# One compressed-attention step a head, staging in the middle of a head, and a scan whose K updates run on VectorE

## The chip, the cores and the metric

The kernel runs on one NeuronCore of a Trainium2 chip. The metric is the device time of one execution in microseconds (us). TensorE (PE) multiplies, VectorE (DVE) and ScalarE (ACT) work elementwise on SBUF and PSUM, GpSimd (POOL) elementwise on SBUF, and SyncE (SP) issues the loads. The engines run their own instruction streams and meet only through semaphores.

## The reference

Two transformer-like blocks run one after the other on a sequence of 512 tokens with 1024 features, all in float32. The first block has a gated feed-forward layer, then a mixed attention, then a second feed-forward layer and a gated embedding. Its attention is what the change touches first: eight "NSA" heads with three branches each (compressed, selected, window) and eight "forgetting" heads.

```python
# compressed branch: 31 blocks of 32 tokens, one key and value per block
s_c = jnp.einsum('bkgqd,bknd->bkgqn', qq, k_cmp) * scale
p_c = masked_softmax(s_c, m_c) * m_c
o_c = jnp.einsum('bkgqn,bknd->bkgqd', p_c.astype(v_cmp.dtype), v_cmp)
...
return gg[..., 0:1] * o_c + gg[..., 1:2] * o_s + gg[..., 2:3] * o_w
```

With 512 tokens there are eight blocks to select and all are taken, so that the selected and the window branch are both plain causal attention over their own keys.

The second block puts 16 meta tokens ahead (528 positions) and runs a gated linear recurrence over them, eight heads of 128:

```python
S_new = jnp.exp(G_last[:, :, 0, :])[..., None] * S + jnp.einsum('bhsd,bhsv->bhdv', k_dec, vb)
```

With decay f, keys are K = 1 - f and the output is a causal sum over earlier positions, each weighted by the product of the decays between them.

## The kernel before

**Layout.** Activations lie transposed, features on the 128 partitions and tokens in the free dimension. Each weight unit is split into two float32r parts: `whi`, made by ScalarE (`hi`, L731), and `wlo`, made by GpSimd in pieces of 128x512 (`lo`, L639). The order of every engine's stream is written out by hand; there is no planner.

**The attention loop** (one loop over `STEPS` in the stream of each engine) has a step for every head n, query block i of 128 queries, and branch b: 0 selected, 1 window, 2 compressed, `FOX` (3) forgetting. That is 8x4x4 = 128 steps. TensorE does in turn s the score of step s (L2093 to L2101), the transposes of the probabilities of step s-2 (L2114, L2117), and the product with the values of step s-4 (L2127, L2131). VectorE takes the row maximum of step s (L1401) and adds up the output of step s-5 into `otok` (L1426 to L1432; the reciprocals and the gates are L1417 and L1419). ScalarE does the exponential (L995) and copies the transposed probabilities to `probT` (L1017, L1019). Scores, transposes and outputs have three, three and two PSUM banks.

A compressed step has 32 keys: a mask product, two score products with `kch` of 32 columns, one transpose to 32 partitions and a product whose operands `probT` and `vcmp` have 32 partitions. A forgetting step has one more score product (L2099), whose operands `negsel` and `csplit` have 40 partitions; it puts the cumulated forget gates on the scores.

**Staging.** Queries and forgetting keys of head n+2 are split into two parts beside the last block of head n: `stage_q` and `stage_fox_q` on ScalarE (L887, L891), `stage_fox_k` (two copies, L1274) and `stage_fox_c` (L1278) on VectorE in one go, the rest on GpSimd (L669, L678).

**The scan** does the recurrence in levels. At level lv, blocks of 2^lv positions are joined in pairs: TensorE forms K transposed times Q for each head (L2248, from level 7 on L2251 and L2254), VectorE selects the part of that level into `Ad` with a predicated copy (L1609, at level -1 L1612), multiplies Q with decays (L1629), and halves the table of decays (L1635, `Tod` and `Tev` in turn); GpSimd multiplies K with decays (L720). The eight heads go as two groups of four. K itself is made by VectorE in one instruction (L1591). The 16 meta positions have small instructions of their own (L1604, L1641 to L1651). The results of levels 7 and 8 are copied by ScalarE (L1099).

Of the kernel before, what the change touches and what calls it, by code (L numbers as in the profile page):

```python
# [6 lines left out]
F32R = mybir.dt.float32r  # L7
# [6 lines left out]
P = 128  # L14
D = 1024
KD = D // P
S = 512
# [88 lines left out]
FOX = 3  # L106
STEPS = [(n, i, b) for n in range(NH) for i in range(TT) for b in (0, 1, 2, FOX)]
# [16 lines left out]
def slot(s):  # L124

    return s % 12
# [19 lines left out]
def level_updates():  # L146

    n, out = 1, {}
# [19 lines left out]
LEVEL_CP0 = sum(lv < 7 for lv, _, _ in LEVEL_SEQ)  # L168
# [6 lines left out]
def build(nc, a, out):  # L175
    ctx = ExitStack()
    with ctx:
# [76 lines left out]
        vcmp = at("vcmp", [32, NKV, HD], R2 + 42752)  # L254
# [10 lines left out]
        negsel = at("negsel", [FL0 + NH, 4, P], AR + U_VW * S * 4, F32R)  # L265
        csplit = at("csplit", [FL0 + NH, S], AR + U_VS * S * 4, F32R)
# [128 lines left out]
        nmax_done = sem("nmax_done")  # L395
        exp_done = sem("exp_done")
# [39 lines left out]
        lev_k = sem("lev_k")  # L436
        amx_mm = sem("amx_mm")
# [193 lines left out]
        def _(pool):  # L631
# [83 lines left out]
            for lv in range(LEVELS - 1):  # L715
                for g in range(2):

                    pool.wait_ge(lev_mm, 1 + max(i for i, (l, n, _) in enumerate(LEVEL_SEQ) if l == lv and n in range(HG * g, HG * (g + 1))))
                    k2, decay = k_update(lv, g)
                    nc.gpsimd.tensor_tensor(k2, k2, decay, ALU.mult).then_inc(lev_k, 1)  # L720
# [4 lines left out]
        def _(act):  # L725
# [220 lines left out]
            act.wait_ge(cmp_mm, 3)  # L946
            nc.scalar.activation(kcsq[:], ps[:, SMALL_BANK, HID0:HID0 + 64], ACT.Square).then_inc(cmp_sq, 1)
            nc.scalar.activation(vcmp[:], ps[0:32, SMALL_BANK, HID0 + 64:HID0 + 192].rearrange("p (g d) -> p g d", g=NKV), ACT.Copy).then_inc(cmp_sq, 1)
# [3 lines left out]
            act.wait_ge(cmp_mm, 4)  # L952
# [9 lines left out]
            nc.scalar.activation(kch[:, 0, :], kcmp[:], ACT.Copy).then_inc(k_hi, 1)  # L962
            nc.scalar.activation(warm[:, 0:1], epsc[:], ACT.Exp).then_inc(warmed, 1)
# [17 lines left out]
            SQ_HEADS = 4 * TT * (NH - 1)  # L981
            SQ0 = SQ_HEADS + LAG_O + 1
            LAST_AT = [SQ_HEADS + 4 * i + LAG_O + 5 - i // 2 for i in range(3)]

            def last_square(n):
                head_square(n, NH - 1, NH, SQ_HEADS + (n // 2 + 1) * 4)

            for s in range(NS + LAG_T):
                if s < NS:
                    n, i, b = STEPS[s]  # L990
                    w = 32 if b == 2 else (i + 1) * P
# [7 lines left out]
                    if i == TT - 1 and n + 2 < NH:  # L999
                        if b == 2:  # L1000
                            stage_q(n + 2)
                        if b == FOX:
                            stage_fox_q(n + 2)
# [1407 lines left out]
```

## Time and profile before

| | us |
|---|---|
| median of 3 runs | 2267.65 |
| lowest and highest | 2264.34, 2269.47 |
| the profiled execution | 2270.92 |
| its span | 2269.1 |

| engine | busy us | share of the span |
|---|---|---|
| PE | 2197.0 | 97% |
| POOL | 931.7 | 41% |
| DVE | 872.5 | 38% |
| ACT | 751.5 | 33% |

In order of time the attention loop lies from 563 to 749 us and the scan from 1687 to 1786 us. What lies around them is projections and feed-forward layers. A busy share says only how long instructions of an engine ran, and not whether they set the time; this is read in each stage from what the engine waited for. The starts of two neighbouring instructions of an engine, one taken from the other, give what the first costs in a full stream; the duration in a row also holds its latency, in which the next one already runs. The granted clock of TensorE is 1.00 at 2.4 GHz and 0.50 at 1.2 GHz.

### The profile page before, as it was taken

The page shows a single profiled execution, that of the slowest core. Times are in us where ns is not written, and L with a number is a line of the kernel's source. Part 1 is how long each engine was busy: PE and PEld are TensorE (multiplying, and loading weights), DVE is VectorE, ACT ScalarE, POOL GpSimd, SP SyncE. Part 2 cuts the span into 40 slices and gives each one's busy share as a digit, 9 for nine tenths or more (in the row PEclk, how much of TensorE's full clock was granted, in tenths as well). Part 3 has the DMA queues.
Part 4 walks back from the last instruction along what each step waited for, and adds up shares of the span by engine and source line. Part 5 has one row for each costly group of instructions (what it writes and reads, how often), then busy time and mean ns, then how long its engine had stood idle before and what let it go on. Part 6 is the DMA issues. An engine that isn't in the chain of part 4 may idle for free.

```text
span 2269.1 us, 32814 instructions
## 1 busy us (share of the span) xinstructions
PE 2197.0 (97%) x12844; PEld 1910.1 (84%) x12844; DVE 872.5 (38%) x1296; ACT 751.5 (33%) x1153; POOL 931.7 (41%) x707
## 2 busy tenths in 40 slices
PE   8999999999999999999999999999988899999998
PEld 6788888777888778887887999999988798989887
DVE  4222202676555432223016322232229554565402
ACT  4333222435666533334124432212210333333213
POOL 3444444435221344444444444444334324454442
PEclk9999999999999999999999999999999999999999
DMA  5323222522000222222322222222210012222321
GB/s 157 94 91 107 87 102 93 151 65 75 1 2 1 65 90 77 93 92 93 111 93 75 75 93 92 87 84 89 93 57 1 20 38 85 83 96 89 105 98 56
DMA packets 152174, 178.98 MB, mean 79 GB/s; under 512 B 6949, under 2 KB 142478, under 8 KB 152094
## 3 DMA queue, kind: packets, MB, share of 16 engines
q1 hardware_dynamic: 151931, 177.83, 24.1%
q8 instruction: 55, 0.90, 0.2%
q14 instruction: 25, 0.20, 0.0%
q10 hardware_dynamic: 163, 0.04, 0.0%
HBM read 175.76 MB, written 2.10 MB: 78 GB/s over the span
## 4 chain that ended last, share of the span: by engine, by line
PE 62%; issue 22%; POOL 11%; DVE 3%; DMA 1%; ACT 0%; SPq 0%; POOLq 0%; DVEq 0%; ACTq 0%
PE ps L1723 40%; POOL wlo L639 11%; PE ps L1863 11%; PE ps L2225 3%; PE ps L2248 2%; PE ps L2131 2%; PE ps L2101 2%; PE ps L2117 1%; PE ps L1975 1%; DVE tmp L1161 1%; DMA raw<-in_ffn_wu 1%; DVE Ad L1609 0%; PE ps L2127 0%; PE ps L2099 0%; PE ps L2182 0%
## 5 line engine op out<-in xcount | busy, mean ns | idle before, releaser
L639 POOL TENSOR_TENSOR wlo<-raw,whi 128x512 fp32r<-128x512 f32 x634 | 831.9, 1344 | 1123.7 <-ACT whi L731 1119.3
L1723 PE MATMUL ps<-xh,whi 128*128 128x512 f32 (+2 forms) x2432 | 703.0, 335 | 10.4 <-POOL wlo L639 8.8
L1723 PE MATMUL ps<-xh,wlo 128*128 128x512 f32 (+2 forms) x2432 | 700.6, 334 | 0.0
L1723 PE MATMUL ps<-xl,whi 128*128 128x512 f32 (+2 forms) x2432 | 697.6, 333 | 0.0
L731 ACT ACTIVATE whi<-raw 128x2048 fp32r<-128x2048 f32 (+1 forms) x158 | 301.1, 1906 | 772.7 <-PE ps L1723 466.8
L1723 PEld LDWEIGHTS ps<-xh,whi 128*128 128x128 f32 x2432 | 415.1, 189 | 62.8 <-POOL wlo L639 10.1
L1723 PEld LDWEIGHTS ps<-xh,wlo 128*128 128x128 f32 x2432 | 414.0, 189 | 46.9 <-issue 1.9
L1723 PEld LDWEIGHTS ps<-xl,whi 128*128 128x128 f32 x2432 | 413.9, 189 | 45.9
L1863 PE MATMUL ps<-act_h,whi 128*128 (+1 forms) x528 | 209.2, 396 | 0.0
L1863 PE MATMUL ps<-act_l,whi 128*128 (+1 forms) x528 | 208.9, 396 | 0.0
L1863 PE MATMUL ps<-act_h,wlo 128*128 (+1 forms) x528 | 208.2, 394 | 0.0
L1220 DVE SCALAR_TENSOR_TENSOR h<-ps,h 128x512 f32<-128x512 f32 x24 | 16.4, 685 | 307.8 <-PE ps L1863 307.3
L1863 PEld LDWEIGHTS ps<-act_l,whi 128*128 128x128 f32 x528 | 99.6, 189 | 23.3
L1863 PEld LDWEIGHTS ps<-act_h,wlo 128*128 128x128 f32 x528 | 99.6, 189 | 23.0
L1863 PEld LDWEIGHTS ps<-act_h,whi 128*128 128x128 f32 x528 | 99.6, 189 | 22.2
L777 ACT ACTIVATE act_h<-tmp 128x512 f32 (+1 forms) x66 | 41.8, 633 | 209.9 <-DVE tmp L1210 209.9
L1207 DVE TENSOR_TENSOR tmp<-ps,rbs 128x512 f32<-128x512 f32 x66 | 45.4, 688 | 148.6 <-PE ps L1723 148.6
L1401 DVE TENSOR_REDUCE stat<-ps 128x1 f32<-128x32 f32 (+4 forms) x128 | 53.0, 415 | 79.4 <-PE ps L2101 78.7
L1188 DVE TENSOR_TENSOR tmp<-ps,rbs 128x512 f32<-128x512 f32 x44 | 30.2, 691 | 135.6 <-PE ps L1723 135.2
L2248 PE MATMUL ps<-Q,K 128*128 128x128 f32 x512 | 65.8, 294 | 15.4 <-DVE Tod L1635 6.4
L995 ACT ACTIVATE prob<-ps,stat 128x32 f32<-128x32 f32 (+4 forms) x128 | 59.7, 466 | 61.8 <-DVE stat L1401 61.4
L2248 PEld LDWEIGHTS ps<-Q,K 128*128 128x128 f32 x512 | 64.2, 208 | 16.6 <-DVE Tod L1635 6.6
(312 smaller groups left out, 2556.0 us busy)
## 6 DMA issues: line engine op xcount, KB each, us to landing
raw<-in_w_in SPq DMA_DIRECT2D x47, 1024.0 KB, 5.1
raw<-in_ffn_wg SPq DMA_DIRECT2D x22, 1024.0 KB, 5.3
raw<-in_ffn_wu SPq DMA_DIRECT2D x22, 1024.0 KB, 5.3
raw<-in_ffn_wd SPq DMA_DIRECT2D x22, 1024.0 KB, 4.9
raw<-in_w_up SPq DMA_DIRECT2D x22, 1024.0 KB, 5.0
raw<-in_w_down SPq DMA_DIRECT2D x11, 1024.0 KB, 4.9
raw<-in_w_out SPq DMA_DIRECT2D x8, 1024.0 KB, 4.9
raw<-in_ple_w_gate SPq DMA_DIRECT2D x4, 1024.0 KB, 5.0
```

The source lines that it names most:

```text
L639: last = nc.gpsimd.tensor_tensor(wlo[:, slot, d], raw[:, slot, d], whi[:, slot, d].bitcast(F32), ALU.subtract)
L731: nc.scalar.activation(whi[:, slot, 0:n], raw[:, slot, 0:n], ACT.Copy).then_inc(hi_ready, 1)
L777: nc.scalar.activation(act_h[:, bass.ds(2 * i + j, 1), :], tmp[:, 2 + j:3 + j, 0:S], ACT.Copy).then_inc(acth_done, 1)
L995: nc.scalar.activation(prob[:, s % 3, 0:w], ps[:, s % 3, 0:w], ACT.Exp, bias=stat[:, 0, slot(s):slot(s) + 1], accum_out=stat[:, 1, slot(s) ...
L1207: nc.vector.tensor_tensor(tmp[:, 2 + j, 0:S], ps[:, 4 + 2 * j if conv else 2 + j, :], rbs[:, M:T], ALU.mult).then_inc(up_scaled, 1)
L1401: nc.vector.tensor_reduce(stat[:, 0, slot(s):slot(s) + 1], ps[:, s % 3, 0:w], AX_X, ALU.max, negate=True).then_inc(nmax_done, 1)
L1723: last = mm(ps[:, j * banks + b, 0:n], w[:, k, e * P:(e + 1) * P], x[:, k, c0:c0 + n], start=(k == 0 and q == 0), stop=(k == KD - 1 and q ...
L1863: last = mm(ps[:, n, :], w[:, e, n * P:(n + 1) * P], x[:, bass.ds(k + e, 1), :].rearrange("p a s -> p (a s)"), start=(start and e == 0 and ...
L2101: last = mm(out_, q_[:, e, i * P:(i + 1) * P], keys[x], start=False, stop=(x == 1), skip_group_check=True)
L2131: last = mm(o, probT[:, q % 3, k, :], vtok[:, k, v0:v0 + 2 * HD], start=(k == 0), stop=(k == i))
L2225: last = mm(ps[:, 3 * (u % 2) + g // 2, g % 2 * UC:(g % 2 + 1) * UC], x[:, k, c0:c0 + P], w[:, k, :], start=(k == 0 and q == 0), stop=(k = ...
L2248: last = mm(ps[:, bank, i * P:(i + 1) * P], K[:, n, xc(i)], Q[:, n, xc(i)], start=True, stop=True)
```

## The change

- The four compressed steps of a head become one, which goes first in the head (`PER_HEAD` is 13, so 104 steps). Its scores lie side by side in 128 columns (eight products of 32 columns and one mask product), VectorE takes four maxima at once, subtracts them from PSUM into `prob`, ScalarE takes one exponential in place, VectorE sums up in blocks, one transpose follows, and one product with `vcmp`, which now has 128 partitions and 256 columns with the values in four diagonal blocks and zeros elsewhere. It writes the compressed branch of all four query blocks to `otok` at once.
- `vcmp` is made by 16 small products in place of 4 in `compressed`, a clearing on VectorE that waits for `k_lo`, and four copies on ScalarE. `negsel` and `csplit` have 128 partitions in place of 40, those beyond filled with zeros.
- Head n+1 is staged inside head n: `stage_q` at step (1, 1), `stage_fox_q` at (2, 0), the two halves of `stage_fox_k` at (2, 1) and (2, FOX), `stage_fox_c` (for n+3) at (3, 0).
- In the scan K is made by ScalarE in two halves, the K updates are VectorE's, between the Q update and the table; TensorE no longer waits for the table; levels 5 and 6 are copied to `Ad` by ScalarE in blocks; GpSimd's next `lo` waits for the last scan product.

```diff
@@ attention, TensorE
-                    if b == 2:
-                        mm(out_, ident_b[:], cmpneg[:, i, :], start=True, stop=False, skip_group_check=True)
-                        keys = [kch[:, x, 32 * it:32 * it + 32] for x in range(2)]
+                    if b == CMP:
+                        mm(out_, ident_b[:], cmpneg[:].rearrange("p i k -> p (i k)"), start=True, stop=False, skip_group_check=True)
+                        for t in range(TT):
+                            for x in range(2):
+                                last = mm(out_[:, 32 * t:32 * t + 32], q_[:, e, t * P:(t + 1) * P], kch[:, x, 32 * it:32 * it + 32],
+                                          start=False, stop=(x == 1), skip_group_check=True)
...
-                    if b == 2:
-                        last = mm(o[:, 0:HD], probT[0:32, q % 3, 0, :], vcmp[:, n // 4, :], start=True, stop=True)
+                    if b == CMP:
+                        if n == 0:
+                            pe.wait_ge(vcmp_ready, TT)
+                        last = mm(ps[:, 6 + q % 2, 0:TT * HD], probT[:, q % 3, 0, :], vcmp[:, n // 4].rearrange("p i d -> p (i d)"),
+                                  start=True, stop=True)
@@ attention, VectorE
+                    if b == CMP:
+                        blocks = lambda x: x.rearrange("p (i k) -> p i k", i=TT)
+                        cmax = cstat[:, 0, TT * (n % 2):TT * (n % 2 + 1)]
+                        nc.vector.tensor_reduce(cmax, blocks(ps[:, s % 3, 0:P]), AX_X, ALU.max, negate=True).then_inc(cmax_done, 1)
+                        dve.wait_ge(cmax_done, n + 1)
...
+                        nc.vector.tensor_tensor(blocks(prob[:, s % 3, 0:P]), blocks(ps[:, s % 3, 0:P]),
+                                                cmax.unsqueeze(2).to_broadcast([P, TT, 32]), ALU.add).then_inc(nmax_done, 1)
...
-                    if b == FOX and i == TT - 1:
-                        if n + 2 < NH:
-                            stage_fox_k(n + 2)
-                        if n + 4 < NH:
-                            stage_fox_c(n + 4)
+                    if 1 <= n < NH - 1:
+                        if (i, b) == (2, 1):
+                            stage_fox_k(n + 1, (0,))
+                        if (i, b) == (2, FOX):
+                            stage_fox_k(n + 1, (1,))
+                        if (i, b) == (3, 0) and n + 3 < NH:
+                            stage_fox_c(n + 3)
@@ scan, ScalarE
+            for g in range(2):
+                heads = slice(HG * g, HG * (g + 1))
+                nc.scalar.activation(K[:, heads, :], Fg[:, heads, :], ACT.Copy, scale=-1.0, bias=1.0).then_inc(k_made, 1)
             for idx, (lv, n, bank) in enumerate(LEVEL_SEQ):
+                if FIRST_CP <= lv < 7:
+                    act.wait_ge(lev_mm, idx + 1)
+                    w = 1 << lv
+                    for r in range(0, P, 2 * w):
+                        last = nc.scalar.activation(Ad[r:r + w, n, :].rearrange("p (i t) -> p i t", i=TT)[:, :, r + w:r + 2 * w],
+                                                    ps[r:r + w, bank, :].rearrange("p (i t) -> p i t", i=TT)[:, :, r + w:r + 2 * w], ACT.Copy)
+                    last.then_inc(lev_cp, 1)
@@ scan, VectorE
-                            if lv:
-                                dve.wait_ge(lev_k, 2 * lv)
+                            k2, decay = k_update(lv, g)
+                            nc.vector.tensor_tensor(k2, k2, decay, ALU.mult).then_inc(lev_k, 1)
+                            dve.wait_ge(lev_k, 2 * lv + g + 1)
@@ scan, TensorE
-                pe.wait_ge(lev_up, 1 if lv < 0 else LEVEL_UP[lv - 1, META if n == META else n // HG])
+                if lv < 0:
+                    pe.wait_ge(k_made, 2 if n == META else n // HG + 1)
+                elif n == META:
+                    pe.wait_ge(lev_up, LEVEL_UP[lv - 1, META])
+                else:
+                    pe.wait_ge(lev_up, LEVEL_UP[lv - 1, n // HG] - (lv > 0))
```

TensorE in the attention loop, around the compressed and the forgetting step of query block 1, before (L2127 and L2099 are the products with 32 and 40 partitions):

```order
L2096 MATMUL ps<-causal,ident_b 128x128
L2101 MATMUL ps<-ksel,qs 128x256 x2
L2117 MATMUL ps<-ident,prob 128x128
L2131 MATMUL ps<-vtok,probT 128x128
L2093 MATMUL ps<-cmpneg,ident_b 128x32
L2101 MATMUL ps<-kch,qs 128x32 x2
L2117 MATMUL ps<-ident,prob 128x128 x2
L2127 MATMUL ps<-vcmp,probT 128x64
L2096 MATMUL ps<-causal,ident_b 128x128
L2099 MATMUL ps<-csplit,negsel 128x256
L2101 MATMUL ps<-whi,wlo 128x256 x2
```

The same place after (line numbers are those of the changed kernel):

```order
L2154 MATMUL ps<-causal,ident_b 128x128
L2159 MATMUL ps<-ksel,qs 128x256 x2
L2172 MATMUL ps<-ident,prob 128x128
L2184 MATMUL ps<-vcmp,probT 128x256
L2154 MATMUL ps<-causal,ident_b 128x128
L2159 MATMUL ps<-ksel,qs 128x256 x2
L2172 MATMUL ps<-ident,prob 128x128
L2189 MATMUL ps<-vtok,probT 128x128
L2154 MATMUL ps<-causal,ident_b 128x128
L2157 MATMUL ps<-csplit,negsel 128x256
L2159 MATMUL ps<-whi,wlo 128x256 x2
```

Between the window and the forgetting step no compressed step is left; its one value product of 256 columns stands in the first turn of query block 1.

VectorE in the scan at level 4 (two groups) and the first group of level 5, before:

```order
L1609 COPY_PREDICATED Ad<-levelmask,ps 128x16x16 x4
L1629 TENSOR_TENSOR Q<-Q,Tev 128x4x16x16
L1635 TENSOR_TENSOR Tod<-Tev 128x64
L1609 COPY_PREDICATED Ad<-levelmask,ps 128x16x16 x4
L1629 TENSOR_TENSOR Q<-Q,Tev 128x4x16x16
L1635 TENSOR_TENSOR Tod<-Tev 128x64
L1609 COPY_PREDICATED Ad<-levelmask,ps 128x8x32 x4
L1629 TENSOR_TENSOR Q<-Q,Tod 128x4x8x32
L1635 TENSOR_TENSOR Tev<-Tod 128x32
```

and after:

```order
L1663 COPY_PREDICATED Ad<-levelmask,ps 128x16x16 x4
L1683 TENSOR_TENSOR Q<-Q,Tev 128x4x16x16
L1686 TENSOR_TENSOR K<-K,Tev 128x4x16x16
L1690 TENSOR_TENSOR Tod<-Tev 128x64
L1663 COPY_PREDICATED Ad<-levelmask,ps 128x16x16 x4
L1683 TENSOR_TENSOR Q<-Q,Tev 128x4x16x16
L1686 TENSOR_TENSOR K<-K,Tev 128x4x16x16
L1690 TENSOR_TENSOR Tod<-Tev 128x64
L1683 TENSOR_TENSOR Q<-Q,Tod 128x4x8x32
L1686 TENSOR_TENSOR K<-K,Tod 128x4x8x32
L1690 TENSOR_TENSOR Tev<-Tod 128x32
```

The K update has come in behind every Q update, and from level 5 on the predicated copies have gone.

## Rows read from the trace of the kernel before

**Rows 1.** Stretches: length, PE, PEld, DVE, ACT, POOL busy (instructions), clock, DMA

```profile
585.00:607.00 22.00, 21.18 (x157) 18.14 (x156) 12.78 (x45) 14.06 (x50) 5.08 (x4) 1.00 0.00 1
...
1687.20:1786.40 99.20, 79.24 (x657) 76.03 (x658) 90.15 (x119) 8.45 (x17) 45.21 (x21) 0.93 0.00 1
...
1747.50:1769.50 22.00, 22.00 (x197) 21.93 (x196) 21.55 (x39) 0.00 (x0) 11.38 (x7) 1.00 0.01 1
```

**Rows 2.** Chain of waits at two head boundaries: start, duration, what

```profile
589.93 1.13 PE ps L2131 x8
...
677.61 1.13 PE ps L2131 x8
```

**Rows 3.** Waits in the loop: in us, times, longest

```profile
PE ps L2131 <- DVE otok L1432: 4.0, 6, 0.8
```

**Rows 4.** Timeline of TensorE in query block 1: start, duration, instruction

```profile
595.81 0.22 PE L2096 MATMUL ps<-causal,ident_b 128*128 128x128 bf16 x1
595.83 0.48 PE L2101 MATMUL ps<-ksel,qs 128*128 128x256 f32 x2
596.16 0.27 PE L2117 MATMUL ps<-ident,prob 128*128 128x128 f32 x1
...
596.73 0.18 PE L2093 MATMUL ps<-cmpneg,ident_b 128*128 128x32 bf16 x1
596.76 0.38 PE L2101 MATMUL ps<-kch,qs 128*128 128x32 f32 x2
596.99 0.44 PE L2117 MATMUL ps<-ident,prob 128*128 128x128 f32 x2
597.53 0.40 PE L2127 MATMUL ps<-vcmp,probT 32*128 32x64 f32 x2
597.86 0.23 PE L2096 MATMUL ps<-causal,ident_b 128*128 128x128 bf16 x1
598.02 0.38 PE L2099 MATMUL ps<-csplit,negsel 40*128 40x256 f32 x1
598.34 0.51 PE L2101 MATMUL ps<-whi,wlo 128*128 128x256 f32 x2
598.68 0.38 PE L2117 MATMUL ps<-ident,prob 128*128 128x128 f32 x2
598.90 0.39 PE L2131 MATMUL ps<-vtok,probT 128*128 128x128 f32 x2
```

**Rows 5.** Timeline of TensorE: the value products of `compressed`

```profile
529.84 0.63 PE L1998 MATMUL ps<-w,hid 128*32 128x64 f32 x8
```

**Rows 6.** Groups of VectorE from 1687.2 to 1786.4: busy us, mean ns, idle before

```profile
L1629 DVE TENSOR_TENSOR Q<-Q,Tod 128x1024 f32<-128x1024 f32 x8 | 15.4, 1924 | 0.8 <-PE ps L2251 0.8
L1629 DVE TENSOR_TENSOR Q<-Q,Tev 128x1024 f32<-128x1024 f32 x8 | 14.5, 1817 | 1.7 <-PE ps L2254 1.6
L1635 DVE TENSOR_TENSOR Tev<-Tod 128x512 f32<-128x512 f32 (+3 forms) x8 | 5.7, 713 | 0.3
...
L1635 DVE TENSOR_TENSOR Tod<-Tev 128x256 f32<-128x256 f32 (+2 forms) x6 | 5.0, 838 | 0.2
L1635 DVE TENSOR_TENSOR Tod<-Fg 128x1024 f32<-128x1024 f32 x2 | 4.9, 2460 | 0.1
...
L1591 DVE TENSOR_SCALAR K<-Fg 128x4224 f32<-128x4224 f32 x1 | 4.3, 4341 | 0.0
```

**Rows 7.** Lines L1629 and L1635: shortest/median/longest in ns, first and last start

```profile
L1629 DVE TENSOR_TENSOR Q<-Q,Tod x8: 1225/1936/2927, 1722.2 to 1776.5; 128x1024 f32<-128x1024 f32 x8
...
L1635 DVE TENSOR_TENSOR Tev<-Tod x8: 168/292/2760, 1723.5 to 1779.5; 128x512 f32<-128x512 f32 x2, 128x128 f32<-128x128 f32 x2, 128x32 f32<-128x32 f32 x2, 128x8 f32<-128x8 f32 x2
```

**Rows 8.** Timeline of the scan: VectorE's first instructions of level 5

```profile
1758.31 1.44 DVE L1609 COPY_PREDICATED Ad<-levelmask,ps 128x256 f32<-128x256 uint8 x4
```

**Rows 9.** Waits from 1687 to 1786

```profile
PE ps L2248 <- DVE K L1591: 5.9, 1, 5.9
```

**Rows 10.** The page's part 5: ScalarE's copies of 128x2048

```profile
L731 ACT ACTIVATE whi<-raw 128x2048 fp32r<-128x2048 f32 (+1 forms) x158 | 301.1, 1906 | 772.7 <-PE ps L1723 466.8
```

More of the change, by code:

```diff
@@ L101, in used_count @@
     return 1 + 2 * (u + 1) + 6 * sum(u >= w for w in (W_DN1 + 10, W_DN2 + 10, W_PLP, W_DN3 + 10))
-FOX = 3
-STEPS = [(n, i, b) for n in range(NH) for i in range(TT) for b in (0, 1, 2, FOX)]
+CMP, FOX = 2, 3
+BRANCHES = (0, 1, FOX)
+STEPS = [step for n in range(NH) for step in [(n, 0, CMP)] + [(n, i, b) for i in range(TT) for b in BRANCHES]]
+PER_HEAD = 1 + len(BRANCHES) * TT
 NS = len(STEPS)
@@ L167 @@
 LEVEL_UP = level_updates()
-LEVEL_CP0 = sum(lv < 7 for lv, _, _ in LEVEL_SEQ)
+FIRST_CP = 5
+LEVEL_CP0 = sum(lv < FIRST_CP for lv, _, _ in LEVEL_SEQ)
 P2 = 5
@@ L714, in _ @@
             nc.gpsimd.memset(Ad[:], 0.0).then_inc(az, 1)
[L715 to L720, printed above, removed]
+            pool.wait_ge(lev_mm, len(LEVEL_SEQ))
             lo_run(W_OUT2 + 1, W_END)
@@ L962, in _ @@
             nc.scalar.activation(kch[:, 0, :], kcmp[:], ACT.Copy).then_inc(k_hi, 1)
+            act.wait_ge(vcmp_zero, 1)
+            for i in range(TT):
+                r = slice(32 * i, 32 * i + 32)
+                nc.scalar.activation(vcmp[r, :, i, :], ps[r, SMALL_BANK, HID0 + 64:HID0 + 192].rearrange("p (g d) -> p g d", g=NKV),
+                                     ACT.Copy).then_inc(vcmp_ready, 1)
             nc.scalar.activation(warm[:, 0:1], epsc[:], ACT.Exp).then_inc(warmed, 1)
@@ L1388, in _ @@
             dve.wait_ge(vtr, 2)
+            nc.vector.tensor_scalar(negsel[:].rearrange("p n q -> p (n q)"), rbs[:, M:T], 0.0, None, ALU.mult).then_inc(fl_v, 1)
+            dve.wait_ge(k_lo, 8)
+            nc.vector.memset(vcmp[:], 0.0).then_inc(vcmp_zero, 1)
+            dve.wait_ge(fl_v, 8)
             for n in range(4):
@@ L2097, in _ @@
                         keys = [kfox[:, e, x, 0:w] if b == FOX else ksel[:, it, b, x, 0:w] for x in range(2)]
[L2098 to L2101 removed]
+                        if b == FOX:
+                            mm(out_, negsel[:, n % 4, :], csplit[:, 0:w], start=False, stop=False, skip_group_check=True)
+                        for x in range(2):
+                            last = mm(out_, q_[:, e, i * P:(i + 1) * P], keys[x], start=False, stop=(x == 1), skip_group_check=True)
                     last.then_inc(score_done, 1)
```

149 lines of the change are left out of this document (84 added, 65 removed).

## The prediction

> **What bounds the kernel now.** I read the page first: TensorE is busy nearly throughout, so only stages in which it waits or does avoidable work can give time. Then I took the two stages that the change touches, as stretches. In a stretch of 22 us inside the attention loop TensorE is busy 21.18, VectorE 12.78 and ScalarE 14.06 us at full clock [rows 1]: the loop is bound by TensorE's stream, and shortening a step's products is what pays. In the scan (99.2 us) it is VectorE: 90.15 us busy against 79.24 of TensorE; between 1747.5 and 1769.5 both are full [rows 1]. Third, the chain of waits gives the length of a head: the same event, the value products after the stall of a head's end, stands at 589.93 and four heads on at 677.61, so a head takes 87.68 / 4 = 21.92 us [rows 2]. Last the timelines give the price of each piece, as differences of starts.
>
> **The attention loop, TensorE.** What a compressed step costs in query block 1: mask and two score products 596.99 - 596.73 = 0.26; its transpose 0.11 (half of the two at 598.68 to 598.90); the value product 597.86 - 597.53 = 0.33; and, ahead of that, TensorE starts two transposes at 596.99 that take 0.22, yet L2127 starts at 597.53, a hole of 0.32 [rows 4]. That makes 1.02, four times a head 4.1 us. The forgetting step pays too: from its mask (597.86) over L2099 to L2101 (598.34) it takes 0.48, where the window step takes 0.02 for the mask and 0.33 / 2 for a product of the same 256 columns, 0.19 [rows 4]. The difference, 0.29, I put down to the operands of 40 partitions and the 32 of L2127 just before; at 128 partitions it goes, 4 x 0.29 = 1.2 us a head. Six times VectorE's staging held up a value product, 4.0 us in all or 0.66 each [rows 3]. Its new places lie in query blocks 2 and 3, one copy at a time, where a turn of TensorE is longest; the cover is VectorE's 9 idle us of 22 [rows 1]. If the cover were gone, the same 0.66 would come back. ScalarE's two copies and GpSimd's parts follow half a head ahead of their use.
>
> What comes in: eight score products at 0.11 (two take 596.76 to 596.99), a mask, one transpose of 0.11, and a value product of 256 columns. One of 128 columns costs about 0.22, as a pair of transposes does (598.68 to 598.90) [rows 4], so 0.44. Sum 0.9 + 0.05 + 0.11 + 0.44 = 1.5 us a head.
>
> Head: 21.9 - 4.1 - 1.2 - 0.66 + 1.5 = 17.4 us if TensorE alone sets it. I add 0.6 us, because the compressed step puts three more instructions into one turn of VectorE (reciprocals, gates and a product of 128x256) just where the turns of query block 1 are shortest: the window turn has 596.73 - 595.81 = 0.92, hole included [rows 4]. The value product two turns on waits for that output. So 18.0, a gain of 3.9. Ends for this term: 17.4 (nothing held up) and 19.5 (a hold of 2 us in each head, three of the old 0.66 us stalls). Over eight heads 8 x 3.9 = 31.2, less 2 x 0.66 since only six heads had the stall, is **-29.9 us**.
>
> The preparation costs: four value products in `compressed` (eight records) take 0.63 us with their latency [rows 5], some 0.55 in the stream; sixteen take 2.2, **+1.7 us**, since TensorE runs without a hole there. Bounds: 0 if a narrower load is cheaper, 3 if each costs as much as a score product pair (12 x 0.23). The clearing of `vcmp` waits for GpSimd's key parts; queued behind it on VectorE are the `negsel` pieces and the evictions of the last two projection tiles, and ScalarE's copies wait with the value evictions behind them. The key parts are done well before and the first forgetting step waits for GpSimd anyway, so I take 0, at most +2.
>
> **The scan, VectorE.** In: 16 K updates. Each has the shape of a Q update, whose shortest is 1.225 us [rows 7]: 16 x 1.22 = +19.5. Out: K itself, 4.3 [rows 6], and 16 predicated copies of levels 5 and 6, 1.44 for four [rows 8], -5.8. And GpSimd's K updates (the bulk of its 45.21 us [rows 1]) run beside VectorE's Q updates, whose median is 1.94 against 1.225 [rows 7]. With GpSimd silent I take the short value: 16 of them went from 15.4 + 14.5 = 29.9 [rows 6] to 19.6, -10.3. The tables: 5.7 + 5.0 + 4.9 = 15.6 [rows 6]; at the median of 0.29 for 14 of them and 1.22 for the two of 1024 elements it is 6.5 [rows 7], -9.1. VectorE's sum: 19.5 - 4.3 - 5.8 - 10.3 - 9.1 = -10.0 us.
>
> Not all of it is time. In levels 0 to 4 VectorE stays the bound and breaks about even: ten K updates (+12.2) against most of the stretch taken off the tables and about half of that off the Q updates. I take 0, between -3 and +3. In levels 5 to 8 VectorE falls to 2 x 1.25 + 0.2 = 2.7 us a group, below TensorE's, whose 192 records of 0.114 in 22 us [rows 1] make 3.65 us a group of 32. There the chain TensorE, Q, K, TensorE is 3.65 + 2.5 a level for two groups of 7.3 in all, so TensorE binds: 4 groups of 3.65, and then level 7 and 8 with short products and 2.5 us of updates between them, some 9.6 us: 24.2, against the 28.1 from 1758.31 [rows 8] to the stretch's end at 1786.4 [rows 1]. **-3.9 us**. The start: TensorE waits 5.9 us for K [rows 9]. After, ScalarE rounds one more weight (1.906 us for 2048 columns [rows 10]), then makes half of K, 2112 columns, in 2.0, so that TensorE waits 3.9. VectorE also has its 4.3 us free. With the low clock after the wait (0.93 over the scan [rows 1]) shorter or as long, that is -2 to -5, taken as **-3 us**. GpSimd's next `lo` comes later, but a whole stage ahead of its use: 0.
>
> A rule of the Trainium skill bears on this: SBUF — State Buffer, on its port side, says that VectorE with two SBUF inputs and GpSimd hold a shared port pair for a whole instruction, the other blocking. The rows show the stretch of 1.94 against 1.225 [rows 7]; by the rule all stretch goes, the sum stays at -7, and the third case below falls away. A second page, TensorEngine Tiling, Key Properties, says a change of tiling mode drains TensorE. The rows show it around L2127 and L2099 only [rows 4]; by the page the transposes to 32 partitions would gain as well, some tenths a head more.
>
> **Sum.** -29.9 + 1.7 - 3.9 - 3.0 = -35.1. The profiled execution took 2270.92 (span 2269.1 and 1.8 around it), so 2235.8; it lies 3.3 above the median 2267.65. Against the median: 2232.5, called 2233.
>
> **Rivals.** (1) *The loop becomes bound by the hand-over between engines*: TensorE's turns get shorter and the steps score, maximum, exponential, transpose don't. For it: a window turn of block 1 has 0.92 us now [rows 4] and 0.2 less without its hole; against it: VectorE and ScalarE at 58% and 64% now [rows 1], some 70% then. Head 19.5: 12 us less gain, 2245.
> (2) *The stall only moves* (the three copies hold VectorE in block 2 as they did at the end): 4.0 us [rows 3], 2237.
> (3) *Q updates stay long* for another reason than GpSimd: VectorE +19.5 - 4.3 - 5.8 = +9.4 instead of -10.0. The scan ends 6 us later than before rather than 7 earlier: 2246. Against: the short ones are there too, down to 1.225 [rows 7].
> (4) *Slower*: the clock. In the loop each us at 1.2 GHz costs half a us. TensorE's holes are few now (21.18 of 22 busy [rows 1]); if the new holes in each head's short turns pull the clock down again and again, 70 us at the low level cost the 35 us gained, and from 79 us on, half of the new loop, it is slower by over 4.5. At 90 us: 2268 - 35 + 45 = 2278. Against: heads now run at 1.00.
> (5) *Better*: no hold, tables and start at their good ends: 17.4 a head and -11 in the scan: 2224.
>
> **How the numbers follow.** Forecast 0.60 (2226 to 2240), (1) 0.14, (2) 0.06, (3) 0.08, (4) 0.04, (5) 0.08. The range goes from 2220 to 2254: the upper end takes in the head of 19.5 with the start of the loop at +2 and the levels at +3, and leaves out (4) and the corner of (1) with (3). 0.2% is 4.5 us, about what a measurement of this kernel can tell from no change. Faster 0.92, same 0.03, slower 0.05.
>
> **What would show it.** A head of 17.4 to 18.5 us between equal value products; no wait of L2131's successor for `otok`; L2157 starting 0.02 after its mask rather than 0.16; Q and K updates at 1.22 to 1.25 throughout and the tables at 1.2 us and less; scan of some 92 us. Wrong would be: heads over 19.5, waits of TensorE for the exponential or `otok` in block 1, Q updates near 2 us with GpSimd silent, or the clock at 0.5 inside the heads.

## The result, and the profile after

| | before | after |
|---|---|---|
| median, us | 2267.78 (4 runs) | 2241.53 (4 runs: 2238.57, 2238.84, 2244.21, 2244.84) |
| ratio to before | | 0.9887 (0.9865 to 0.9908) |
| the profiled execution | 2270.92 | 2238.84 |
| its span | 2269.1 | 2236.9 |

The change makes the kernel 26 us faster, 1.1%. Predicted were 2233 with a range from 2220 to 2254, so by medians the saving is 9 us smaller than forecast. I compare the profiled executions stage by stage, each stage from one event to the same event in the other trace. The last column is a second trace of the same changed kernel (e0 in the experiments): where it differs from the first, the difference is not the change's.

| stage | before, us | after, us | difference | predicted | difference in e0 |
|---|---|---|---|---|---|
| attention loop: first forgetting step to the wait ahead of the output's transposes | 568.55 to 752.43 | 570.09 to 731.87 | -22.1 | -29.9 | -22.5 |
| everything ahead of the value products of `compressed` (code not touched on TensorE) | 529.84 | 531.37 | +1.5 | 0 | -0.4 |
| from there to the loop | 529.84 to 568.55 | 531.37 to 570.09 | 0.0 | +1.7 | 0.0 |
| loop to scan (code not touched) | 752.43 to 1685.84 | 731.87 to 1661.66 | -3.6 | 0 | -0.3 |
| scan: last eviction of V to the first meta score | 1685.84 to 1786.35 | 1661.66 to 1755.47 | -6.7 | -6.9 | -6.5 |
| from there to the end (code not touched) | 1786.35 to 2269.1 | 1755.47 to 2236.9 | -1.3 | 0 | +0.1 |

What both traces share is -22 in the loop and -6.6 in the scan, 29 in all against 35 forecast. The heads of the attention loop gave 7.5 us less than forecast, and `compressed` cost 1.7 us less. The rows of untouched code differ by up to 3.6 us in one trace and by 0.4 at most in the other, so I put them down to chance. The last 3 us between these 29 and the 26 by medians are not located; the profiled execution of before was itself 3.3 us above its median.

First the stretches of after, for [rows 1] (length, then busy us and instructions of PE, PEld, DVE, ACT, POOL, then granted clock and DMA). The first lies in the heads, the second is the scan.

```profile
585.00:605.00 20.00, 18.23 (x149) 16.98 (x148) 13.50 (x42) 13.03 (x43) 5.06 (x4) 1.00 0.01 1
1662.70:1755.00 92.30, 75.27 (x656) 71.62 (x656) 78.86 (x118) 19.77 (x43) 3.21 (x2) 0.98 0.00 1
```

TensorE, which was busy 96% of a stretch of the heads before, is now busy 91%: the loop is shorter, but it is no longer TensorE's stream alone that sets it. The clock in the heads is 1.00 as before. What TensorE waits for in the loop (in us, times, longest), against [rows 3]:

```profile
PE ps L2189 <- DVE otok L1487: 9.0, 6, 1.5
PE ps L2189 <- ACT probT L1030: 2.3, 5, 0.6
```

(Two more waits, of 3.7 and 2.3 us, stand at the loop's two ends and were there before.) The first row is new in size: before, six waits of the value products for VectorE's output took 4.0 us, now six take 9.0. Just ahead of it VectorE is at L1428, the product of two reciprocals with two gates, 128x2 elements. The timeline of VectorE, GpSimd and the value products around one of the six:

```profile
617.31 0.77 DVE L1297 CAST whi<-uT 64x512 fp32r<-64x512 f32 x1
618.22 2.60 POOL L679 TENSOR_TENSOR whi<-uT,whi 64x512 fp32r<-64x512 f32 x2 [0.43 <-DVE whi L1297]
618.32 1.18 DVE L1428 TENSOR_TENSOR stat<-stat,gsig 128x2 f32<-128x2 f32 x1
619.54 0.28 DVE L1487 SCALAR_TENSOR_TENSOR otok<-ps,stat,otok 128x64 f32<-128x64 f32 x1
619.97 0.68 PE L2189 MATMUL ps<-vtok,probT 128*128 128x128 f32 x4 [1.51 <-DVE otok L1487]
```

The second key copy (L1297) ends at 618.08 and releases GpSimd's two key parts (L679) at 618.22. A tenth of a microsecond later VectorE reaches its gate product, and this one takes 1.18 us. The line's shortest, median and longest show how odd that is:

```profile
L1428 DVE TENSOR_TENSOR stat<-stat,gsig x26: 160/161/1208, 594.3 to 716.1; 128x2 f32<-128x2 f32 x26
```

It ends when the first of GpSimd's two pieces has ended (618.22 + 2.60 / 2 = 619.52). Then the output follows, and the value product that needed its bank free has waited 1.51 us.

The places that the prediction named as gains look as forecast. The forgetting step's gate product starts 0.03 us behind its mask (0.16 in [rows 4]) and the value product of the compressed step costs 611.64 - 611.21 = 0.43:

```profile
609.33 0.22 PE L2154 MATMUL ps<-causal,ident_b 128*128 128x128 bf16 x1
609.36 0.31 PE L2157 MATMUL ps<-csplit,negsel 128*128 128x128 f32 x1
609.50 0.39 PE L2159 MATMUL ps<-whi,wlo 128*128 128x128 f32 x2
609.73 0.29 PE L2172 MATMUL ps<-ident,prob 128*128 128x128 f32 x1
...
611.21 0.60 PE L2184 MATMUL ps<-vcmp,probT 128*128 128x256 f32 x2
611.64 0.22 PE L2154 MATMUL ps<-causal,ident_b 128*128 128x128 bf16 x1
```

In the scan, the groups of VectorE (busy us, mean ns, idle before), against [rows 6], and TensorE's wait for K, against [rows 9]:

```profile
L1686 DVE TENSOR_TENSOR K<-K,Tod 128x1024 f32<-128x1024 f32 x8 | 9.8, 1226 | 0.3
L1683 DVE TENSOR_TENSOR Q<-Q,Tev 128x1024 f32<-128x1024 f32 x8 | 9.8, 1221 | 5.0 <-PE ps L2317 3.2 <-PE ps L2311 1.7
```

```profile
PE ps L2311 <- ACT K L1109: 4.0, 1, 4.0
```

Q and K updates are at 1.22 to 1.23 us where the Q updates had means of 1.82 and 1.92, and the wait for K is 4.0 instead of 5.9.

### The profile page after: what moved, and what is told of

It is laid out like the page before. It is cut to its first block, busy times and chain, and to the rows that moved or that the text cites. A ratio compares the mean times of both kernels' runs of the same rounds, so it can differ in the third digit from the quotient of the medians.

```text
span 2236.9 us, 32464 instructions
## 1 busy us (share of the span) xinstructions
PE 2160.2 (97%) x12772; PEld 1887.6 (84%) x12772; DVE 866.1 (39%) x1281; ACT 751.5 (34%) x1102; POOL 894.9 (40%) x691
## 4 chain that ended last, share of the span: by engine, by line
PE 62%; issue 21%; POOL 11%; DVE 4%; DMA 1%; ACT 0%; SPq 0%; POOLq 0%; DVEq 0%; ACTq 0%
PE ps L1778 40%; PE ps L1918 11%; POOL wlo L649 11%; PE ps L2283 3%; PE ps L2189 2%; PE ps L2311 2%; PE ps L2159 1%; PE ps L2172 1%; PE ps L2030 1%; DVE tmp L1184 1%; DMA raw<-in_ffn_wu 1%; DVE Ad L1663 0%; DVE stat L1448 0%; PE ps L2240 0%; PE ps L2317 0%
## 5 line engine op out<-in xcount | busy, mean ns | idle before, releaser
L2189 PE MATMUL ps<-vtok,probT 128*128 128x128 f32 x480 | 71.9, 281 | 13.5 <-DVE otok L1487 9.0
L2189 PEld LDWEIGHTS ps<-vtok,probT 128*128 128x128 f32 x480 | 61.6, 193 | 18.1 <-issue 14.0
L1576 DVE TENSOR_TENSOR tmp<-ps,rbs 128x528 f32<-128x528 f32 x32 | 22.6, 707 | 134.0 <-PE ps L1778 134.0
```

Source lines behind the costliest of these rows:

```text
L1576: nc.vector.tensor_tensor(dst, bank2(j), by, ALU.mult).then_inc(p2_lin, 1)
L2189: last = mm(o, probT[:, q % 3, k, :], vtok[:, k, v0:v0 + 2 * HD], start=(k == 0), stop=(k == i))
```

## Experiments

To compare the loop of several kernels I take one event that occurs once a head, VectorE's maximum over the compressed scores (`cstat`). For after the line reads

```profile
L1441 DVE TENSOR_REDUCE cstat<-ps x8: 290/292/292, 566.1 to 703.6; 128x4 f32<-128x128 f32 x8
```

The first head is no fair measure. In every kernel of this study the clock falls to its lower level for some time between 565 and 580 us, and by how much varies from run to run: over the first head its mean is 0.91 in e0, 0.83 in after and 0.76 in e1, and that head took 19.4, 19.7 and 21.3 us. So a head is here the second start to the last, divided by six; but for e3 (0.88) and e8 (0.97) the clock is 1.00 over that stretch. The second start of after, and both ends in e1:

```profile
585.87 0.29 DVE L1441 TENSOR_REDUCE cstat<-ps 128x4 f32<-128x128 f32 x1 [0.72 <-PE ps L2151]
...
585.51 0.29 DVE L1441 TENSOR_REDUCE cstat<-ps 128x4 f32<-128x128 f32 x1 [0.73 <-PE ps L2151]
694.03 0.29 DVE L1441 TENSOR_REDUCE cstat<-ps 128x4 f32<-128x128 f32 x1 [0.73 <-PE ps L2151]
```

So a head takes (703.56 - 585.87) / 6 = 19.61 us in after and (694.03 - 585.51) / 6 = 18.09 in e1. The kernels ran on more than one chip; each stands beside the kernel before on its own chip (medians 2267.64 for e0 to e3, 2267.01 for e4 to e7, 2269.4 for e8 and e9, 9 to 11 runs each), and the ratios are what I compare.

| kernel | median, us | ratio (95%) | a head, us |
|---|---|---|---|
| e0_after | 2242.20 | 0.9891 (0.9876 to 0.9906) | 19.61 |
| e1_moved | 2233.47 | 0.9854 (0.9839 to 0.9869) | 18.09 |
| e2_poollate | 2234.73 | 0.9853 (0.9838 to 0.9868) | 18.82 |
| e3_endstage | 2259.33 | 0.9967 (0.9953 to 0.9981) | 22.43 |
| e4_best | 2226.88 | 0.9823 (0.9810 to 0.9835) | 17.92 |
| e5_narrow | 2252.29 | 0.9935 (0.9923 to 0.9948) | 20.91 |
| e6_oldscan | 2248.42 | 0.9906 (0.9892 to 0.9919) | 19.63 |
| e7_kpool | 2245.21 | 0.9905 (0.9890 to 0.9919) | 19.62 |
| e8_endlate | 2248.47 | 0.9912 (0.9899 to 0.9926) | 20.09 |
| e9_bestlate | 2230.45 | 0.9826 (0.9813 to 0.9839) | 17.92 |

My theory (A) was that GpSimd's key parts block VectorE's two-input product, and that this is the 1.5 us a head. The rival (B) was that the short turns simply hold too much of VectorE's work, so that the hold moves with the work and not with GpSimd.

**The changed kernel again**, as the common base.

> The changed kernel as it is, beside the three variants of this call. Theory A (GpSimd's key parts block a two-input VectorE instruction through a shared resource) and theory B (the hand-over in short turns, or the staging copies themselves, hold the loop) both expect heads of 19.6 us in the attention loop and about 2240 us.

2242.2, within the spread of the first four runs, and heads of 19.61 us again.

**The second key copy and the gate row one place later in the head.** The copy that releases GpSimd then no longer stands just ahead of a gate product.

```diff
-                        if (i, b) == (2, FOX):
+                        if (i, b) == (3, 0):
                             stage_fox_k(n + 1, (1,))
-                        if (i, b) == (3, 0) and n + 3 < NH:
+                        if (i, b) == (3, FOX) and n + 3 < NH:
                             stage_fox_c(n + 3)
```

> The second half of the forgetting key's copy goes from step (2, FOX) to (3, 0), and the negated selection from (3, 0) to (3, FOX); nothing else. GpSimd's two key parts (2.6 us) then start behind the reciprocal and gates of the same turn and end before those of query block 3's turn. Theory A: the 1.5 us hold of each of six heads goes, heads 18.1 us, 9 us less than the changed kernel. Theory B: the same copies stand one turn later, so at most 1 to 2 us less in all.

8.7 us faster than e0, and a head takes 18.09 us instead of 19.61, as theory A had it (18.1). The waits for `otok` at L1487 are gone from the list, and a stretch of the heads that had 18.23 us of TensorE in 20 now has

```profile
585.00:605.00 20.00, 19.71 (x162) 18.49 (x162) 12.74 (x44) 13.87 (x44) 5.09 (x4) 1.00 0.01 1
```

with the same work on every engine. Only its place on VectorE has moved.

**GpSimd alone held back**, with VectorE's order untouched.

```diff
                 q_lo_of(n, qfox, U_QF, fox_q_hi, fox_q_lo)
+                if n >= 2:
+                    pool.wait_ge(o_done, PER_HEAD * (n - 1) + 5)
                 k_lo_of(2 * n, e, ...
```

> VectorE's and ScalarE's streams are those of the changed kernel; GpSimd alone waits, ahead of its two key parts for heads 2 to 7, until VectorE has the output of the fourth step but last behind it, so that the gates of that turn are past. Theory A: the hold on the gates of query block 2 goes; since the parts now begin beside the negated selection of the next turn, up to one new block of 1.3 us there, with more slack; 3 to 9 us less than the changed kernel. Theory B: no change, or up to 1 us more for the wait.

7.5 us faster than e0. Here VectorE does exactly what it does in the changed kernel and at the same places, and only the start of GpSimd's pieces is another. The waits at L1489 (L1487 in after) fall from 9.0 to 2.8 us. That decides between A and B: most of the hold belongs to GpSimd. A head falls by 0.8 us only, half of what e1 brought; the pieces now meet the `negsel` row, as theory A said (0.98 us at 618.05, against 0.27 when GpSimd is silent).

**Staging at the head's end, as before the change**, all else as after.

```diff
+                    if b == FOX and i == TT - 1:
+                        if n + 2 < NH:
+                            stage_fox_k(n + 2)
+                        if n + 4 < NH:
+                            stage_fox_c(n + 4)
```

(ScalarE's two query copies stand at the head's end again too.)

> The third part of the change undone: queries and keys of head n+2 are staged beside the last query block of head n, as before; one compressed step a head and the new scan stay. Theory A: the old stall of 0.66 us returns in six heads and that of 1.5 us goes: 5 us less than the changed kernel. Theory B, that staging in the middle helps as was meant and the hold comes from elsewhere: 4 us more than the changed kernel.

17 us slower than e0, far outside both. The timeline at a head's end tells why:

```profile
607.11 1.26 POOL L688 TENSOR_TENSOR qs<-uT,qs 64x512 fp32r<-64x512 f32 x1 [17.93 <-ACT qs L892]
607.35 1.76 DVE L1297 CAST whi<-uT 64x512 fp32r<-64x512 f32 x2
609.08 1.26 POOL L688 TENSOR_TENSOR wlo<-uT,wlo 64x512 fp32r<-64x512 f32 x1 [0.71 <-ACT wlo L896]
609.15 1.27 DVE L1301 TENSOR_SCALAR negsel<-negones,headsel 40x128 fp32r<-40x128 f32 x1
...
610.42 2.61 POOL L679 TENSOR_TENSOR whi<-uT,whi 64x512 fp32r<-64x512 f32 x2
610.54 1.16 DVE L1428 TENSOR_TENSOR stat<-stat,gsig 128x2 f32<-128x2 f32 x1
...
612.16 1.62 PE L2187 MATMUL ps<-vtok,probT 128*128 128x128 f32 x6 [3.05 <-DVE otok L1485]
```

Three of VectorE's instructions in a row meet a GpSimd piece: the casts, the `negsel` row (0.27 us when GpSimd is silent) and the gate product. This hold is 3.05 us. The six holds of the loop are 2.80, 3.05, 2.81, 3.05, 1.47 and 1.71 us:

```profile
PE ps L2187 <- DVE otok L1485: 14.9, 6, 3.0
```

A second cost comes on top. TensorE's clock is 1.00 up to the hold of 612.16 and near its lower level of 1.2 GHz behind it (first row: length, PE busy, clock, DMA). The same comes behind all six, also behind the two short ones; the next two rows are the hold of 1.47 us and what follows it (with all engines, as in [rows 1]), and the last is the stretch from the second to the last head:

```profile
610.60:617.40 6.80, 5.24 (x25) 0.54 0.01 2
...
682.21 1.07 PE L2187 MATMUL ps<-vtok,probT 128*128 128x128 f32 x6 [1.47 <-DVE otok L1485]
...
683.00:686.00 3.00, 3.00 (x17) 2.94 (x16) 0.48 (x2) 1.47 (x4) 1.33 (x2) 0.50 0.00 0
...
588.10:722.70 134.60, 120.28 (x850) 112.42 (x851) 81.84 (x242) 77.91 (x238) 26.44 (x21) 0.88 0.01 1
```

The six holds of 1.5 us in the changed kernel have none of this (1.00 in the heads). So a head at 22.43 is 2.8 us longer than 19.61: the hold is 2.5 us on average instead of 1.5, which is 1.0 of it. The rest, 1.8 us a head, I put down to the low clock, which is an estimate: some 29 us of TensorE's work ran at the lower level, and at half speed that loses up to 14 us, or 2.4 a head. The staging in mid-head, which I had priced at 0.66 us a head, is worth 17 us in a kernel with one compressed step a head, and more of this is the clock than the longer hold.

**The same with GpSimd's key parts held back** (the wait of e2 added to e3).

> Staging at the end of a head as in e3_endstage, and GpSimd's key parts held back until the fifth step of the head before the one that reads them, as in e2_poollate; GpSimd's parts of the queries still follow their staging at the head's end. Theory A (the 17 us that end staging cost were VectorE's copies blocked by GpSimd's pieces, and the low clock behind each hold): the key copies run unblocked, the hold of 3.0 us a head falls to 0.5 to 1.5 us and the low clock behind it goes: 2233 to 2243. Theory B (two copies and a gate row in the short turns of a head's end are too much by themselves): the hold stays at 2 us or more, 2250 to 2260.

By ratios 12 of the 17 us come back (head 20.09 instead of 22.43, clock 0.97 instead of 0.88 over the same heads), but it stays 5 us slower than the changed kernel, which is between the two theories. The waits for `otok` are now

```profile
PE ps L2189 <- DVE otok L1487: 11.0, 6, 2.1
```

Both theories had a part: without the key parts the gate product is short again, but the casts and the `negsel` row still meet GpSimd's query parts at the head's end, and this leaves a hold of 2.1 us. The six holds are 1.82, 2.06, 1.82, 2.07, 1.47 and 1.72 us, and the clock fell behind two of them, the second and the fifth. The fourth and the fifth, each with the clock behind it:

```profile
649.29 0.91 PE L2189 MATMUL ps<-vtok,probT 128*128 128x128 f32 x6 [2.07 <-DVE otok L1487]
...
649.50:652.00 2.50, 2.50 (x25) 2.48 (x25) 0.84 (x4) 1.74 (x5) 0.00 (x0) 1.00 0.00 0
...
668.84 1.62 PE L2189 MATMUL ps<-vtok,probT 128*128 128x128 f32 x6 [1.47 <-DVE otok L1487]
...
670.00:672.00 2.00, 2.00 (x12) 1.94 (x11) 0.48 (x2) 0.60 (x4) 0.00 (x0) 0.50 0.00 0
```

So the longer hold left the clock up and the shorter one brought it down.

**e1_moved with the compressed step's gates computed earlier.** The chain reciprocal, gates, product of the compressed step stood in one short turn; its first two links are ready two turns before.

```diff
+                if 3 <= s < NS + 3 and STEPS[s - 3][2] == CMP:
+                    n = STEPS[s - 3][0]
+                    c = TT * (n % 2)
+                    dve.wait_ge(csum_done, n + 1)
+                    weigh(cstat, c, c + TT, c, gsig[:, :, 3 * n + GATE_OF[0]])
                 if s >= LAG_O:
...
                     if b == CMP:
                         c = TT * (n % 2)
-                        dve.wait_ge(csum_done, n + 1)
-                        weigh(cstat, c, c + TT, c, gsig[:, :, 3 * n + GATE_OF[0]])
```

> Both edits of e1_moved (the second key copy and the gate row one place later in the head), and the reciprocal and gate product of the compressed step issued two turns earlier on VectorE, where its sums are just ready, so that only the 128x256 product is left in the short turn of query block 1. Theory A (what was left of the hold in a head is the chain reciprocal, gates, product in one short turn): the wait of the value product for that output, 0.4 to 0.6 us a head, goes, 0.2 to 0.5 us a head or 2 to 4 us against e1_moved, so about 2231. Theory B (after e1_moved TensorE's own stream sets the head): no change against e1_moved, within 1 us, 2233 to 2234.

2226.88, the fastest kernel of this study, 6.6 us below e1 by medians and 7.0 by ratios. A head takes 17.92 instead of 18.09, which is just under what A said for one head (0.2 to 0.5) and makes 1.4 us over eight. The two profiled executions differ by 2.4 us; the first head is 2.8 shorter, with a mean clock of 0.91 over it against 0.76, which is chance. So the traces show 1 to 2 us for this edit. The intervals of the two ratios leave the difference between some 3 and 11 us; where the rest of the 7 comes from is open. Of the waits for VectorE's output one of 0.2 us is left inside the loop, beside four for ScalarE's evictions (2.0 us in all):

```profile
PE ps L2192 <- DVE otok L1490: 0.2, 1, 0.2
```

**And with GpSimd held back as well.**

> The three edits of e4_best, and GpSimd's key parts held back as in e2_poollate. Theory A (in e4_best what is left of the holds, 0.2 us in some heads, is not GpSimd's): same as e4_best within 2 us, 2225 to 2229. Theory B (GpSimd's key parts still cost there): 2 to 4 us less, 2223 to 2225.

The same as e4 by ratios (0.9826 against 0.9823) and by the head (17.92 in both); the median of 2230.45 is that of another chip. Nothing of the block is left to take.

**The gate-score product with 40 partitions again.** The other 88 hold zeros, so the sums are the same.

```diff
-                            mm(out_, negsel[:, n % 4, :], csplit[:, 0:w], ...
+                            mm(out_, negsel[0:FL0 + NH, n % 4, :], csplit[0:FL0 + NH, 0:w], ...
```

> The changed kernel with the gate-score product reading 40 partitions of its two operands again instead of 128 (the other 88 are zero, so the same sums). Theory A (the prediction's: the 40-partition operands cost part of the 0.29 us a step): the step from the mask to the end of the score products takes 0.13 to 0.3 us more in each of the 32 forgetting steps, +4 to +9 us, 2246 to 2251. Theory B (the 0.29 us came from the 32-partition products ahead of it, which are gone): the gate product costs the same, 2241 to 2243.

10 us slower than the changed kernel (0.9935 against 0.9891), at A's upper end by ratios and 1 us above it by the median. The same step as above, in this kernel:

```profile
611.49 0.22 PE L2154 MATMUL ps<-causal,ident_b 128*128 128x128 bf16 x1
611.64 0.32 PE L2157 MATMUL ps<-csplit,negsel 40*128 40x128 f32 x1
611.89 0.44 PE L2159 MATMUL ps<-whi,wlo 128*128 128x128 f32 x2
612.17 0.30 PE L2172 MATMUL ps<-ident,prob 128*128 128x128 f32 x1
```

From mask to transpose it takes 0.68 us where after takes 0.40. Four times 0.28 is 1.1 us of the 1.30 that a head is longer (20.91 - 19.61). The Trainium skill, TensorEngine Tiling (Array Packing), Key Properties, says that a change of tiling mode drains TensorE. The trace doesn't say in which mode a product of 40 partitions runs; if it is another one, the rows agree, on both sides of L2157: 0.15 instead of 0.03 us ahead of it, 0.25 instead of 0.14 behind.

**The whole scan as before**, with the new attention: K made by VectorE, K updates on GpSimd, levels 5 and 6 copied by VectorE.

> The changed attention with the whole scan as before: K made by VectorE, K updates on GpSimd, VectorE copying levels 5 and 6. From the trace of the changed kernel the stretch from the eviction of the scan's values to the meta scores went from 100.5 to 93.8 us, so theory A (the two halves of the change add up): +6.7 us, about 2249, and the scan's stretch back at 100 to 101. Theory B (part of the scan's gain is the clock that a shorter wait left behind, and varies by run): +4 to +9.

The scan's stretch is 1663.23 to 1765.1, 101.9 us against 93.8, and its clock is 0.92 against 0.98. By medians the kernel is 6.2 us slower than e0, by ratios 3.4, and its five runs spread from 2241.8 to 2249.9. The sign and the size agree with 6.7; more exactly these runs can't say it.

**Only the K updates back on GpSimd**, with ScalarE still making K and copying levels 5 and 6.

```diff
+                    k2, decay = k_update(lv, g)
+                    nc.gpsimd.tensor_tensor(k2, k2, decay, ALU.mult).then_inc(lev_k, 1)
...
-                            k2, decay = k_update(lv, g)
-                            nc.vector.tensor_tensor(k2, k2, decay, ALU.mult).then_inc(lev_k, 1)
-                            dve.wait_ge(lev_k, 2 * lv + g + 1)
+                            if lv:
+                                dve.wait_ge(lev_k, 2 * lv)
```

> The changed kernel with only the 16 K updates moved back to GpSimd; ScalarE still makes K and copies levels 5 and 6. Theory A (two-input operations of VectorE and GpSimd with operands in SBUF hold each other up): the Q updates' median goes from 1.23 back to 1.9 us or more and the decay tables' from 0.3 to 0.9, so VectorE loses 19.5 us of K updates and gets some 18 to 20 back as stretch; levels 0 to 4 within 2 us, later levels 0 to 4 us longer since K arrives after a GpSimd update of 2.9 us: 2242 to 2247. Theory B (the stretch had another cause): Q updates stay at 1.23, VectorE is 19 us lighter, and the scan gets 5 us shorter or more: 2237 or less.

3.2 us slower than e0 by ratios, inside A's range, and the scan is 97.0 us (1664.37 to 1761.4) against 93.8. The form of the expectation was wrong: the median of the Q updates stayed at 1.23, because here most of GpSimd's updates begin behind them and meet the decay tables. But what does meet is held until GpSimd's piece is over, whether large or small:

```profile
1743.13 1.91 POOL L732 TENSOR_TENSOR K<-K,Tev 128x1024 f32<-128x1024 f32 x1 [1.65 <-PE ps L2318]
1743.19 2.94 DVE L1691 TENSOR_TENSOR Q<-Q,Tev 128x1024 f32<-128x1024 f32 x1 [0.39 <-PE ps L2318]
...
1751.89 2.62 POOL L732 TENSOR_TENSOR K<-K,Tod 128x1024 f32<-128x1024 f32 x1 [0.43 <-PE ps L2321]
1752.79 1.75 DVE L1697 TENSOR_TENSOR Tev<-Tod 128x8 f32<-128x8 f32 x1
```

The first Q update starts 0.06 us behind GpSimd and takes 2.94, about the rest of GpSimd's piece (1.85) and its own 1.23. The table product of eight elements a partition, 0.17 us in the changed kernel, takes 1.75: it ends at 1754.54, GpSimd's piece at 1754.51. Over the scan VectorE is busy 84.48 us without the K updates and 78.86 with them. So theory A's cause is shown, and its form was not.

## Why the prediction was right and where it was not

**The bound** was read rightly in both stages. In the loop TensorE's stream was what a shorter step paid into, and in the scan it was VectorE.

**The head** was put at 18.0 us and took 19.6, above the term's own upper end of 19.5. Two of the prediction's signs of being wrong came true, a head over 19.5 and waits for `otok`. The step that failed is the sentence on the staging: "If the cover were gone, the same 0.66 would come back. ScalarE's two copies and GpSimd's parts follow half a head ahead of their use." It asked whether GpSimd's parts would be late, and not whom they block while they run. The cover of "9 idle us of 22" was there, and did not help, because the instruction behind the copies was blocked and not queued. The hold came back as 1.5 us instead of 0.66. The trace of before had the same meeting, in a place where it fell into slack: VectorE's gate product beside a piece of GpSimd's that began just ahead of it takes 0.82 us.

```profile
591.32 2.61 POOL L669 TENSOR_TENSOR whi<-uT,whi 64x512 fp32r<-64x512 f32 x2
591.78 0.82 DVE L1419 TENSOR_TENSOR stat<-stat,gsig 128x3 f32<-128x3 f32 x1
```

Term by term the sum was 17.4 as the base, 0.6 for the compressed step's chain on VectorE, and nothing for a hold. The runs show 17.92 (e4), 0.17 (from e1 to e4) and 1.52 (from e0 to e1). That e4's 17.92 lies so near the forecast 18.0 is luck: the base was 0.5 too low and the chain 0.4 too high.

**The base** was too low because the compressed step was priced in query block 1 and taken four times. By the same differences in the trace of before it costs 0.88, 1.02, 0.95 and 0.87 us in blocks 0 to 3, 3.7 instead of 4.1 in all, since the hole ahead of its value product is smaller elsewhere. In block 3 it is 607.99 - 607.41 - 0.44 = 0.14 instead of 0.32:

```profile
607.15 0.18 PE L2093 MATMUL ps<-cmpneg,ident_b 128*128 128x32 bf16 x1
607.41 0.66 PE L2117 MATMUL ps<-ident,prob 128*128 128x128 f32 x4
607.99 0.43 PE L2127 MATMUL ps<-vcmp,probT 32*128 32x64 f32 x2
608.35 0.23 PE L2096 MATMUL ps<-causal,ident_b 128*128 128x128 bf16 x1
```

The rest is small waits, 0.2 to 0.3 us a head, that e4 still has.

**The operands of 40 partitions** were priced at 1.2 us a head, and e5 measured 1.3.

**Six and two.** The sum over eight heads missed less than 8 x 1.6 = 13 us: the loop is 22.1 us shorter, not 29.9. The block is there in six heads only, since the first and the last stage nothing.

**`compressed`** was mis-sized. It was put at +1.7 and cost about 0.1: the sixteen value products take 531.99 - 531.37 = 0.62 us where four took 0.55.

```profile
531.37 0.69 PE L2054 MATMUL ps<-w,hid 128*32 128x64 f32 x32
531.99 0.50 PE L1778 MATMUL ps<-xh,whi 128*128 128x512 f32 x1
```

The loop of after does start 1.5 us later, but this difference is there ahead of these products already, and in e0 it is -0.4. The wait for the cleared `vcmp` at the start of the loop added nothing, as forecast.

**The scan** (-6.9) came as -6.7, and -6.5 in e0, nearly term by term. Levels 0 to 4 went from 51.6 us to 1730.70 - 1679.14 = 51.6, for 0 predicted. Levels 5 to 8 went from 28.0 to 1755.47 - 1730.70 = 24.8, -3.3 for -3.9. The start went from 20.9 to 1679.14 - 1661.66 = 17.5, -3.4 for -3. The rows around the starts of level 0 and of level 5 after, on VectorE:

```profile
1679.14 2.45 DVE L1663 COPY_PREDICATED Ad<-levelmask,ps 128x256 f32<-128x256 uint8 x4
...
1730.70 1.22 DVE L1683 TENSOR_TENSOR Q<-Q,Tod 128x1024 f32<-128x1024 f32 x1
```

One reading in that sum has another source than the row it names: 192 records in 22 us are those of L2248 alone, where [rows 1] has 197 with all of TensorE's. And the ends that the prediction adds up for the range (a head of 19.5, +2, +3) give 2250, not 2254.

**What looked like a further gain** in the profiled execution is chance: -3.6 us between loop and scan, and -1.3 behind it, where no code differs. Right behind the loop the clock was 0.91 from 740 to 760 before, and 1.00 from 718 to 738 after; the sixteen transposes there took 3.57 us before and 1.97 after. In e0 they took 3.48 us, and the two stretches differ from before by -0.3 and +0.1. The four runs of after lie in pairs, near 2238.7 and near 2244.5; one of them has a trace, so what parts the pairs isn't shown.

**The rivals.** (1) gave the head nearly its length (19.5) for another reason: TensorE doesn't wait for scores, maximum or exponential, as e1 shows, and the list of waits has 2.3 us for ScalarE's evictions and none of note for the exponential. (2) had the right place, staging in block 2, and the wrong price and mechanism: not three copies that hold VectorE, but one GpSimd piece that they release. (3) fell: Q updates at 1.22 to 1.23 us. (4), the clock, did not happen in the changed kernel, but e3 shows that it can: behind each of its six holds the clock fell, over the heads to a mean of 0.88, and together with the longer holds that took 17 of the 25 us gained. (5) was too good by the head alone.

## What to carry to other kernels

When a step is moved, look not only at when its products are needed but at which engine it sets going and what stands next in the other engine's stream: here a copy released two GpSimd pieces exactly ahead of a tiny product on VectorE, and one place later it did not, which was worth 8.7 us. An idle share is no cover against a block, which strikes the instruction that comes next however small it is. And where several small instructions form a chain in the shortest turn of a pipeline, take out of that turn what is ready earlier (0.17 us a head here, by the traces). Last, before a difference between two traces is explained, look whether a second trace of the same kernel shows it, and leave out stretches in which the clock varies by run.

## What the runs showed of the hardware

VectorE's two-input products in SBUF and GpSimd's hold each other up, and how long doesn't depend on the size of what is held. A product of 128x2 elements, 0.16 us alone, takes up to 1.21 us, and one of 128x8 takes 1.75 instead of 0.17. It isn't restricted to two-input products either: the cast of 64x512 took 0.42 us when GpSimd was silent and 0.77 beside one, and `negsel` (a scalar product of 40x128) 0.27 and 1.27. Maxima and predicated copies from PSUM kept their times beside GpSimd: 0.56 us for the maximum at 616.72 in after, beside the piece that began at 616.52, and 1.43 us for four copies both at 1751.04 in before, beside GpSimd's update of 1751.40, and at 1726.60 in after with GpSimd silent. The Trainium skill, SBUF — State Buffer, Who interferes with whom, says of the first three: two SBUF inputs contend with a GpSimd instruction that reads SBUF, copies, casts and scalar operations can do so in their two-port modes, and reductions never on this chip. The rows agree; I had weighed that rule in the scan only, and the loop is where it cost.

The clock fell behind some holds of TensorE and not behind others, and the length of the hold doesn't tell which. It stayed at 1.00 behind all six of 1.5 us in after and behind one of 2.07 in e8; it fell to 0.50 behind those of 1.47 in e3 and in e8, for some 3 us, and behind the four of 2.8 to 3.05 in e3, for some 6 us. The wait of 3.68 us at the loop's end was followed by sixteen transposes in 1.97 us in after and in 3.48 in e0, by the same code. What decides is open.
